# Three products of each weight block side by side, with both weight parts awaited in front of every unit

## The reference

```
proj = h @ w_in                      # first block, 1024 -> 3404
x = x + rmsnorm(mix @ w_out, g)
m = square(relu(h @ w_up)) @ w_down  # 1024 -> 4096 -> 1024
x = x + sigmoid(x @ w_ple_gate) * (p_i @ w_ple_proj)

z = x @ w_in + b_in                  # second block, 1024 -> 11648
merged = sigmoid(gate_a) * (y_a @ w_attn_proj) + sigmoid(gate_b) * (y_b @ w_ret_proj)
x = layer_norm(ALPHA * x + merged @ w_out)
x = layer_norm(ALPHA * x + (silu(x @ w_gate) * (x @ w_up)) @ w_down)
```

## Time and profile before

| What | Value |
|---|---|
| Median of three runs | 2215.45 us |
| Profiled execution, first to last instruction | 2223.9 us |
| Time of the profiled execution beside its span | not given; the span stands 8.45 us over the median |
| PE busy | 2102.3 us (95%), 9270 matmuls |
| PEld busy | 1704.1 us (77%), 9270 loads |
| DVE busy | 1195.4 us (54%) |
| ACT busy | 874.2 us (39%) |
| Mean granted TensorE clock | 0.909 of full speed |

### The profile page before, as it was taken

One profiled execution on the slowest core, in us unless ns is written; L12 is line 12 of the kernel. 1 busy time (PEld: TensorE's weight loads), 2 busy tenths in 40 slices (PEclk: granted clock), 3 DMA queues, 4 the chain that ended last, 5 costly groups with the idle time before them and its releaser, 6 DMA issues.

```text
span 2223.9 us, 26315 instructions
## 1 busy us (share of the span) xinstructions
PE 2102.3 (95%) x9270; PEld 1704.1 (77%) x9270; DVE 1195.4 (54%) x1360; ACT 874.2 (39%) x997; POOL 62.0 (3%) x88
## 2 busy tenths in 40 slices
PE   4999999989989998999999998997999999998997
PEld 3877788777778886877877787886877887787885
DVE  3655654556555455533657556455533657556455
ACT  3532444455234445321335433443321335433442
POOL 2210000022000000000000000000000000000000
PEclk9978999999579998975999999998975999999998
DMA  6413455543035554555355654555555355653553
GB/s 195 153 37 100 152 189 179 176 157 101 1 119 189 183 175 142 187 147 139 128 174 176 221 173 137 177 181 177 191 144 137 128 173 173 220 176 126 186 179 113
DMA packets 214819, 345.17 MB, mean 155 GB/s; under 512 B 13355, under 2 KB 82219, under 8 KB 214721
## 3 DMA queue, kind: packets, MB, share of 16 engines
q1 hardware_dynamic: 213440, 342.10, 48.2%
q0 software_dynamic: 384, 1.31, 0.2%
q10 hardware_dynamic: 897, 0.49, 0.1%
HBM read 342.74 MB, written 1.12 MB: 155 GB/s over the span
## 4 chain that ended last, share of the span: by engine, by line
PE 92%; issue 3%; DVE 2%; ACT 1%; DVEq 1%; POOL 0%; DMA 0%; POOLq 0%; ACTq 0%; SPq 0%
PE G L573 21%; PE G L574 21%; PE G L579 20%; PE T L598 6%; PE A L573 3%; PE A L574 3%; PE A L579 3%; PE G L714 3%; PE G L691 3%; PE G L717 2%; PE A L641 2%; PE A L646 2%; ACT arena L1001 1%; PE A L904 0%; DVEq L1869 0%
## 5 line engine op out<-in xcount | busy, mean ns | idle before, releaser
L1380 DVE TENSOR_TENSOR wlo<-raw,whi 128x2048 fp32r<-128x2048 f32 (+3 forms) x320 | 676.3, 2115 | 661.2 <-ACT whi L1001 661.0
L1001 ACT ACTIVATE whi<-raw 128x2048 fp32r<-128x2048 f32 (+3 forms) x320 | 565.9, 1769 | 788.6 <-PE G L579 717.1
L573 PE MATMUL G<-whi,XH 128*128 128x512 f32 x1696 | 679.9, 401 | 6.6 <-DVE XL L1395 6.6
L574 PE MATMUL G<-whi,XL 128*128 128x512 f32 x1696 | 669.2, 395 | 0.0
L579 PE MATMUL G<-wlo,XH 128*128 128x512 f32 x1696 | 419.1, 389 | 0.0
L573 PEld LDWEIGHTS G<-whi,XH 128*128 128x128 f32 x1696 | 324.9, 192 | 77.1 <-issue 6.5
L574 PEld LDWEIGHTS G<-whi,XL 128*128 128x128 f32 x1696 | 324.4, 191 | 67.9 <-issue 1.9
L579 PEld LDWEIGHTS G<-wlo,XH 128*128 128x128 f32 x1696 | 318.3, 188 | 66.5 <-DVE wlo L1380 0.4
L598 PE MATMUL T<-ident,arena 128*128 128x128 f32 x812 | 140.1, 319 | 12.2 <-ACT arena L1001 5.4
L1001 ACT ACTIVATE arena<-G,nm 128x128 f32<-128x128 f32 (+2 forms) x104 | 50.3, 493 | 231.3 <-DVE nm L1421 151.2
L598 PEld LDWEIGHTS T<-ident,arena 128*128 128x128 f32 x812 | 112.0, 165 | 28.8 <-ACT arena L1001 10.1
(11 more groups left out here) (189 smaller groups left out, 1959.5 us busy)
## 6 DMA issues: line engine op xcount, KB each, us to landing
raw<-in_w_in SPq DMA_DIRECT2D x112, 1024.0 KB, 6.9
raw<-in_w_mlp_up SPq DMA_DIRECT2D x32, 1024.0 KB, 5.3
raw<-in_w_mlp_down SPq DMA_DIRECT2D x32, 1024.0 KB, 5.0
raw<-in_w_ffn_gate SPq DMA_DIRECT2D x44, 512.0 KB, 4.1
raw<-in_w_ffn_up SPq DMA_DIRECT2D x44, 512.0 KB, 5.0
raw<-in_w_ffn_down SPq DMA_DIRECT2D x44, 512.0 KB, 3.3
raw<-in_w_out SPq DMA_DIRECT2D x16, 1024.0 KB, 5.0
raw<-in_w_ret_proj SPq DMA_DIRECT2D x16, 1024.0 KB, 5.0
```

The lines of the kernel that those rows point to most:

```text
L573: nc.tensor.matmul(dst(m), hx[:, k0 + k, rows], hi[:, k, :], start=first and k == 0, stop=False)
L574: nc.tensor.matmul(dst(m), lx[:, k0 + k, rows], hi[:, k, :], start=False, stop=False)
L1001: return nc.scalar.activation(out_, in_, func, **kw)
L1380: tt(wlo[:, c % PARTS, 0:n], raw[:, slot, 0:n], whi[:, c % PARTS, 0:n].bitcast(F32), ALU.subtract).then_inc(s_lo.sem, 1)
```

## The change

Each unit has one loop over its weight blocks and token tiles in place of two, and in it the three products of a block and tile follow each other: XL with whi, XH with whi, XH with wlo. Both waits, for `s_hi` and for `s_lo`, stand in front of the first product. In units with `halves` the order is by token tile in all three products, so `s_half` is raised after half of the unit. The number of products is the same, and nothing changes on the other engines.

```diff
                 pe.wait_ge(s_hi.sem, s_hi.at(blk, L, 4 * i + c + 1))
-                for k in range(kb):
-                    for m in range(TILES):
-                        rows = slice(m * P, (m + 1) * P)
-                        nc.tensor.matmul(dst(m), hx[:, k0 + k, rows], hi[:, k, :], start=first and k == 0, stop=False)
-                        nc.tensor.matmul(dst(m), lx[:, k0 + k, rows], hi[:, k, :], start=False, stop=False)
                 pe.wait_ge(s_lo.sem, s_lo.at(blk, L, 4 * i + c + 1))
                 order = [(k, m) for m in range(TILES) for k in range(kb)] if halves else \
                     [(k, m) for k in range(kb) for m in range(TILES)]
                 for k, m in order:
-                    mm = nc.tensor.matmul(dst(m), hx[:, k0 + k, m * P:(m + 1) * P], lo[:, k, :],
-                                          start=False, stop=last and k == kb - 1)
+                    rows = slice(m * P, (m + 1) * P)
+                    nc.tensor.matmul(dst(m), lx[:, k0 + k, rows], hi[:, k, :], start=first and k == 0, stop=False)
+                    nc.tensor.matmul(dst(m), hx[:, k0 + k, rows], hi[:, k, :], start=False, stop=False)
+                    mm = nc.tensor.matmul(dst(m), hx[:, k0 + k, rows], lo[:, k, :], start=False,
+                                          stop=last and k == kb - 1)
                     if halves and (k, m) == (kb - 1, 0):
                         mm.then_inc(s_half.sem, 1)
```

## The result

The changed kernel takes 2286.18 us, median of 4 runs (2279.43 to 2287.80); the kernel before has 2216.51 (2207.74 to 2221.32, 4 runs). The ratio is 1.0305, 95% interval [1.0276, 1.0334]. Forecast were 2284 us, slower, with a range from 2262 to 2304.

The account below looks back on a forecast made before the run. PE was taken to bound the kernel, so its added waits count almost in full. Stops at late wlo, restarts and clock loss summed to 68.2 us: 2215.45 + 68.2 = 2284 us, range 2262 to 2304 for 8 in 10.

Parts of the forecast that it names:

- What bounds: Whole kernel: PE's chain ended last for 92%, so whatever PE waits in addition is added to the time almost in full.
- Order of the products at 0: All 7080 products: the new order costs 0, spacing being the same; bounds 95 us of gain and 7 us of loss.
- Cover of 1.00 us in steady units: Full units following full units: weight parts are ready 1.00 us before the next unit starts, so the moved wait costs nothing.
- Feed-forward loop: Second block, full unit after a half-size one: PE starts 1.35 us late each turn, 18 times, 24.3 us.
- the 61 told: Expected sign in the changed profile: PE idle until DVE's wlo ends, in 18 places and six, some 61 us in all.
- First units and gate: Six first units after X is turned wait for wlo, 24.2 us; unit 51 delays the gate, 3.2; restarts 0.3.
- Rotation: Beside DVE's rotation work, wlo of units 18, 20, 22 is late; only 18 and 22 pay, 4 x 1.13 = 4.5 us.
- Attention unit at 0: First block's attention: one unit a layer is 0.5 us late beside a DVE chain; counted as 0, at most 1.0.
- Clock: Six stops after transposes: idle PE falls to half rate, 5.4 us on top; bounds -3 to +25.
- Earlier s_half at 0: Units with `halves`: the first half is free 8 products sooner; counted as 0, at most 2 us of gain.

## Why the prediction was right

- *What bounds.* PE's time is the kernel's time: 72.7 us of growth read at PE's starts, and 1.0305 to 1.0324 timed. The sum of 68.2 was 4.5 us short of that growth; that the median came within 3 us of the 2284 owes something to the scatter of the attention stretches, which is larger than either difference.
- *Order of the products at 0.* Shown twice, by the old order with early waits and by the new order with the waits met. The bounds, -95 to +7, were far wider than what the chip did: 0.227 us from product to product in all kinds.
- *Cover of 1.00 us in steady units.* It held in all of them: no full unit behind a full unit stops in the MLP loop, whose turn moved by 0.01.
- *Feed-forward loop.* 1.42 for 1.35 + 0.05. As idle time it shows with 1.15 in the trace and not with the 1.3 to 1.4 told, and the six first units with 3.6 to 4.3 and not 3.8 to 4.6, since an idle time is counted from a modelled end; the 58.8 us in all are near the 61 told. The tie of each turn's whi to PE's start of unit 69 is what makes it come back 18 times.
- *First units and gate.* 29.2 for 27.7. The excess is at the second gate: unit 51 ran at half rate there, 4.86 us from first to last product for 2.65 in layer 0, a place that was not among the clock's in the prediction.
- *Rotation.* Only units 18 and 22 pay, as forecast; taking all three late units would have given 6.8 for the measured 4.7.
- *Attention unit at 0.* The one term whose reasoning failed: unit 11's 0.58 us shows in PE's starts up to unit 13 and is not absorbed. 1.2 us in all.
- *Clock.* 6.6 for 5.4, with 1.0, 2.3, 1.3, 0.4, 0.0 and 1.7 for the six. The mean was near and the single places were not to be forecast; with bounds from -3 to +25 the nearness is in part luck.
- *Earlier s_half at 0.* No stretch behind a `halves` unit became shorter beyond the clock's scatter. It was not tried alone.

What the forecast didn't know was the scatter of the attention stretches, of up to 16 us a stretch. It lies within the stated range and does not touch the sign.

## What to carry to other kernels

A wait that moves forward costs, unit by unit, how late its operand is at the new place, and nothing where it is early; so compare the producer's end with the consumer's start for each unit, not in the mean (DVE was 54% busy here). With two buffers the producer is tied to the consumer, so small units ahead of big ones and work that stands first in the producer's queue are the places to look at. Then ask of each late unit whether the tie makes the loss return in every turn, as behind a half-size unit, or lets the next one find its operand ready, as beside the rotation.

## What the runs showed of the hardware

Stretches that keep PE busy for 94 of 95.7 us were granted 0.55 in both kernels. They hold products of 64 to 256 columns, those of the logits in part over 64 rows, and transposes. With 4 dropped products of 128x512 a job they were granted 0.84 and 0.98, with 10 a job 1.00, and became up to 21 us shorter although they hold more work. The Trainium skill says of transposes that they do not count as busy in the same way ("TensorE: Matmul & The Clock Gate", "Part 4: PE-mode transpose"), which fits; no run here tells the transposes' part from that of the thin products. A few dense products among thin ones lift the rate of all. Busy time is not work: at half rate the same work shows double.

The first block's attention, with the same instructions, took 64.1 to 79.9 us by a granted clock from 0.75 to 0.55. Runs of the kernel before fall accordingly: where the mean clock of a run is on record, those at 0.915 to 0.919 took 2209 to 2216 us, and those at 0.909 to 0.912 took 2221 to 2226. What decides which of them an execution gets stays open. For a difference under 0.5% in such a kernel, compare the stretches that the change touches rather than the totals.
